# Two heads' half-array products of a linear attention issued in turn, and the whole-array products of its output put ahead of them

## What is computed

```python
def step(state, xs):
    qc, kc, vc, bc = xs
    o_inter = jnp.einsum('bhcd,bhde->bhce', qc * jnp.exp(bc), state)
    diff = bc[:, :, :, None, :] - bc[:, :, None, :, :]
    decay = jnp.exp(jnp.where(causal[:, :, None], diff, -jnp.inf))
    attn = jnp.einsum('bhid,bhjd,bhijd->bhij', qc, kc, decay)
    o_intra = jnp.einsum('bhij,bhje->bhie', attn, vc)
    b_last = bc[:, :, -1:, :]
    k_dec = kc * jnp.exp(b_last - bc)
    state = jnp.exp(b_last[:, :, 0, :])[..., None] * state + jnp.einsum('bhcd,bhce->bhde', k_dec, vc)
    return state, o_inter + o_intra
```

## Time and profile before

| | |
|---|---|
| median of 3 runs | 869.12 us (868.48 to 869.97) |
| profiled execution, its own time | 872.03 us |
| profiled execution, span of the trace | 870.2 us |
| mean granted TensorE clock in it | 0.993 |
| PE busy (share of span) | 848.4 us (97%) |
| DVE busy | 658.6 us (76%) |
| ACT busy | 556.8 us (64%) |
| POOL busy | 242.0 us (28%) |
| HBM traffic | 145 MB, 167 GB/s over the span |

### The profile page before, as it was taken

The page is one execution under the profiler, slowest core; times in us unless marked ns, Lnnn a source line. Parts: engine busy times, 40 slices in busy tenths (PEclk is TensorE's granted clock), DMA queues, the critical chain, the costliest instruction groups (busy, mean ns, idle before and its releaser), DMA issues.

```text
span 870.2 us, 16608 instructions
## 1 busy us (share of the span) xinstructions
PE 848.4 (97%) x6016; PEld 793.7 (91%) x6016; DVE 658.6 (76%) x1171; ACT 556.8 (64%) x1015; POOL 242.0 (28%) x252
## 2 busy tenths in 40 slices
PE   8999989999999999999999999999999999999996
PEld 8998989999999999999889888999998888888885
DVE  7998999996878897877766658837589766656552
ACT  7778969886746676666455685466646665555441
POOL 2387833332322153333101100010022152222111
PEclk9999999999999999999999999999999999999998
DMA  7665553534455476555656543335345465565731
GB/s 262 215 205 181 164 164 122 155 126 150 158 184 190 121 219 192 180 184 170 224 169 191 161 153 121 122 123 169 121 146 186 142 208 192 184 181 169 230 131 49
DMA packets 43024, 146.12 MB, mean 168 GB/s; under 512 B 4912, under 2 KB 7232, under 8 KB 42944
## 3 DMA queue, kind: packets, MB, share of 16 engines
q1 hardware_dynamic: 42336, 144.52, 52.6%
q10 hardware_dynamic: 608, 0.55, 0.2%
HBM read 144.00 MB, written 1.05 MB: 167 GB/s over the span
## 4 chain that ended last, share of the span: by engine, by line
PE 73%; DVE 12%; issue 4%; POOL 4%; ACT 4%; DMA 2%; DVEq 0%; SPq 0%; POOLq 0%; ACTq 0%
PE px L539 20%; PE px L543 12%; PE px L544 12%; PE px L545 12%; PE px L540 10%; DVE wlo L1400 4%; POOL CA L2011 4%; DMA raw<-ws 2%; PE px L588 2%; DVE px L1500 2%; PE px L610 1%; DVE hx L1417 1%; PE px L756 1%; ACT whi L899 1%; PE px L611 1%
## 5 line engine op out<-in xcount | busy, mean ns | idle before, releaser
L1400 DVE TENSOR_TENSOR wlo<-raw,whi 128x1024 fp32r<-128x1024 f32 x265 | 334.1, 1267 | 27.7 <-ACT whi L899 27.4
L899 ACT ACTIVATE whi<-raw 128x1024 fp32r<-128x1024 f32 x265 | 277.8, 1052 | 57.5 <-PE px L540 28.2
L543 PE MATMUL px<-hx,whi 128*128 128x256 f32 x1024 | 296.4, 289 | 2.8 <-DVE wlo L1400 1.6
L544 PE MATMUL px<-hx,whi 128*128 128x256 f32 x1024 | 290.1, 283 | 0.0
L545 PE MATMUL px<-hx,wlo 128*128 128x256 f32 x1024 | 290.0, 283 | 0.0
L543 PEld LDWEIGHTS px<-hx,whi 128*128 128x128 f32 x1024 | 196.7, 192 | 5.4 <-issue 2.8
L544 PEld LDWEIGHTS px<-hx,whi 128*128 128x128 f32 x1024 | 196.8, 192 | 0.4
L545 PEld LDWEIGHTS px<-hx,wlo 128*128 128x128 f32 x1024 | 196.6, 192 | 0.0
L2011 POOL TENSOR_TENSOR CA<-CA,ct 128x256 f32<-128x256 f32 x90 | 91.9, 1021 | 98.0 <-ACT ct L994 53.9
L539 PE MATMUL px<-fx,whi 128*128 128x512 f32 x330 | 115.6, 393 | 0.0
L539 PE MATMUL px<-hx,whi 128*128 128x512 f32 x320 | 113.4, 399 | 0.8 <-DVE wlo L1400 0.5
(11 more groups left out here) (315 smaller groups left out, 1378.7 us busy)
## 6 DMA issues: line engine op xcount, KB each, us to landing
raw<-ws SPq DMA_DIRECT2D x265, 512.0 KB, 3.6
tb<-tabs SPq DMA_DIRECT2D x16, 128.0 KB, 2.3
X<-xs SPq DMA_DIRECT2D x4, 256.0 KB, 3.7
raw<-ws SPq DMA_DIRECT2D x4, 256.0 KB, 5.0
out<-X SPq DMA_DIRECT2D x4, 256.0 KB, 2.4
vc<-vecs SPq DMA_DIRECT2D x1, 315.5 KB, 6.4
msk<-lmask ACTq DMA_DIRECT2D x1, 256.0 KB, 2.7
ug<-pos ACTq DMA_DIRECT2D x1, 128.0 KB, 3.9
```

The source lines that it names most:

```text
L543: e.matmul(b[:, 0:S], H, xh, start=first, stop=False)
L544: e.matmul(b[:, 0:S], H, xl, start=False, stop=False)
L899: e.activation(whi[:, n % NSL, :], raw[:, n % NRAW, :], ACT.Copy).then_inc(s_hi, 1)
L1400: e.tensor_tensor(wlo[:, n % NSL, :], raw[:, n % NRAW, :], whi[:, n % NSL, :], ALU.subtract).then_inc(s_lo, 1)
```

## The change

Only PE's program changes, in three of the helpers above. In `products` the loop over `par` goes inside, so that the two halves of the array are addressed in turn, matmul by matmul. In `chunk_sums` the order is written out: (p_, ci) = (0,0), (0,1), (1,0), (1,1), (0,2), (1,2). In `linear_out` the 8 whole-array matmuls of both `par` go first, and then the 12 half-array ones follow, with `par` changing at every matmul. Semaphore updates stay on the last matmul of what they announce. The number of instructions, their operands and their banks are the same.

```diff
-                for par in range(2):
-                    o = 64 * par
-                    for i in range(4):
-                        p_, t = i // 2, i % 2
+
+                for i in range(4):
+                    p_, t = i // 2, i % 2
+                    for par in range(2):
+                        o = 64 * par
                         if n == 0:
                             m = e.matmul(bs[par][:, i * P:i * P + P], gk[o:o + 64, p_, t * P:t * P + P],
...
-                for ci in range(3):
+                for p_, ci in ((0, 0), (0, 1), (1, 0), (1, 1), (0, 2), (1, 2)):
                     o, t = 64 * (ci % 2), ci // 2
-                    for p_ in range(2):
-                        m = e.matmul(bs[ci][:, p_ * S:p_ * S + S], kd[o:o + 64, t, p_ * P:p_ * P + P],
-                                     gv[o:o + 64, t, p_ * S:p_ * S + S], start=(p_ == 0), stop=True, skip_group_check=True)
-                    m.then_inc(s_cu, 1)
+                    m = e.matmul(bs[ci][:, p_ * S:p_ * S + S], kd[o:o + 64, t, p_ * P:p_ * P + P],
+                                 gv[o:o + 64, t, p_ * S:p_ * S + S], start=(p_ == 0), stop=True, skip_group_check=True)
+                    if p_ == 1:
+                        m.then_inc(s_cu, 1)
...
                 for par in range(2):
-                    b, o = bs[par], 64 * par
+                    b = bs[par]
                     for p_ in range(2):
                         h = 2 * p_ + par
                         for t in range(2):
                             e.matmul(b[:, p_ * S + t * P:p_ * S + t * P + P], gv[:, t, h * P:h * P + P],
                                      at[:, par, (2 * p_ + t) * P:(2 * p_ + t) * P + P],
                                      start=(p_ == 0 and t == 0), stop=False, skip_group_check=True)
-                    for p_ in range(2):
-                        for ci in range(1, 4):
-                            m = e.matmul(b[:, p_ * S + ci * 64:p_ * S + ci * 64 + 64], gs[o:o + 64, ci - 1, p_, :],
+                for p_ in range(2):
+                    for ci in range(1, 4):
+                        for par in range(2):
+                            o = 64 * par
+                            m = e.matmul(bs[par][:, p_ * S + ci * 64:p_ * S + ci * 64 + 64], gs[o:o + 64, ci - 1, p_, :],
                                          qL[o:o + 64, p_, ci * 64:ci * 64 + 64], start=False, stop=True,
                                          skip_group_check=True)
-                    m.then_inc(s_go, 1)
+                            if p_ == 1 and ci == 3:
+                                m.then_inc(s_go, 1)
```

## The result

The changed kernel takes 864.88 us (median of 6 runs, 863.64 to 865.93) against 868.86 us for the kernel before (6 runs, 868.16 to 872.45) measured beside it: ratio 0.9949, 95% interval 0.9933 to 0.9965. A repeat in a later session gave 0.9959 (0.9943 to 0.9975), with medians of 866.66 and 868.90 us. One of its twelve executions took 1169.47 us at a mean granted clock of 0.654 and is left out of that ratio. The forecast was 865.2 us, 0.45% faster.

A forecast was written before the change was run, and what follows sets the result against it. PE was taken as the bound, busy 97% of the span. Savings of 2.24 (`products`) + 0 (`chunk_sums`) + 1.67 (`linear_out`) = 3.9 us off 869.12 gave 865.2 us; forecast's own range 864.4 to 866.0, wider range 863.2 to 867.6.

The forecast's parts named there:

- The price of a pass and the pairing: In `products`, a pass takes a 0.112 us slot; both halves run together, 8 slots not 12, saving 0.45 us a call.
- The first two calls bring nothing: `products(0)` and `products(1)`: 0.9 us of PE's gain lost waiting for DVE; wait before `products(2)` about 1.26 us.
- From `products(2)` on the gain stays: Five later `products` calls keep 0.448 us each, 2.24 us; tightest is `products(6)`, with about 1.1 us left.
- `chunk_sums` at nothing: In `chunk_sums` upper passes already run beside lower ones, so reordering gains nothing; bounds 0.22 us more or less.
- `linear_out`, 3.36 us: `linear_out` falls from 5.03 to 3.36 us, saving 1.67, with 24 half-array passes in 12 slots.
- The clock: Half-clock stretch from 529.86 us, costing 1.5 us, expected to stay; rivals: gone, 863.7 us (0.12); another, 866.7 us (0.10).
- Draining at each switch: Rival: each switch of half on the path costs 0.09 us, 43 times, without pairing; about 875 us, chance 0.04.
- no pairing: Rival: alternating halves gives one pass a slot or little better, 12 slots a `products` call; 868.8 us, chance 0.07.
- Strict program order: Rule for MATMUL starts: old `products` call 16 slots, 1.8 us; change saves about 5.8 us in all; given no chance.

## Why the prediction held

- *The price of a pass and the pairing.* Right: 8 slots in place of 12, and the kernel with turns of 1 to 4 matmuls shows the reach of four passes that I had read from the earlier trace rows. The saving is 0.46 to 0.49 us a call, not 0.448: the upper half's first pass now shares the slower first slots with the lower half's too.
- *The first two calls bring nothing.* Right, and shown alone: ratio 1.0009, wait 1.28 us where about 1.26 was forecast. What is lost there is 1.0 us and not 0.9, since `products(0)`, with moving operands of 128 columns, saves 0.55 us.
- *From `products(2)` on the gain stays.* Right in the sum, 2.4 us against 2.24. The tightest case was not `products(6)`, as I wrote, but `products(3)`: in the change its queries are ready at 530.80 (below, the timeline of DVE) and PE comes at 531.51, 0.7 us later.

```profile
530.38 0.42 DVE L1840 TENSOR_TENSOR go<-gq,eb 128x256 f32<-128x256 f32 x1
```

  In the earlier trace rows that place was covered by the stretch at half clock, which held PE back, and I took its slack from a profile that had it. The two runs that moved calls on PE ran into just this.
- *`chunk_sums` at nothing.* Right, 1.92 us both times.
- *`linear_out`, 3.36 us.* Right, 3.37 (forecast saving 1.67, measured 1.66).
- *The clock.* "So I expect the same half-speed stretch" was wrong for the profiled execution: its profile has neither that stretch nor the one near 120 us, and a changed number of stretches was among the prediction's own signs of being wrong. The price was right, 1.49 us against 1.5. The argument from the sum of idle and half-array time, 2.3 us both ways, does not hold: with that sum the same the stretch was there in one profile of the change and not in the other. I should have asked how often it comes rather than whether.
- *The nearness of the number.* 864.88 us lies 0.3 us from the forecast, and that is partly luck. One stretch more or less is worth 1.5 us, and in the repeat the medians were 866.66 and 868.90 us, 2.2 us apart, while the ratio gives 3.6 us. What does not depend on it is the saving in the passes, 4.08 us against the forecast 3.9.
- *Draining at each switch, and no pairing.* Neither: 24 passes in turns take 1.49 us (562.26 to 563.75), as twelve of one half did (1.48). The 0.09 us that the draining rival starts from is the way from half to whole array and not, as written, from whole to half: the five passes from 567.24 are half-array ones with a whole-array one behind the earlier trace rows.
- *Strict program order.* With turns of four matmuls a call takes 1.53 us in place of the 1.8 that sixteen slots need. The Trainium skill, "TensorE: Matmul & The Clock Gate", Part 3, says that MATMULs start in strict program order. For products of different halves the trace disagrees with that again.

## What to carry to other kernels

The fp32 matmuls here that fill only the lower or the upper 64 rows run side by side if the program offers the other half's pass within about four passes, so order such matmuls in turns, or at most in pairs (in `products` and `linear_out` each half has a bank of its own; a shared one was not tried). Keep whole-array matmuls together, apart from them. Before adding up such savings, strike out those in front of a wait for another engine: here 1.0 of 3.4 us of `products` was lost there, and it took a reordering on DVE, not on PE, to remove that wait without a new one. Differences between two single profiles (6.7 us here) can hold stretches of half clock that have nothing to do with the change (two of them here, 1.5 us each); compare the distances between marked instructions.

## What was not expected of the hardware

Entering the half array and leaving it again costs 0.34 us (3.71 against 3.37 us), as much as three passes. And the stretch at half clock behind `products(2)` starts 1.4 to 2.0 us after that call begins when it comes at all (529.86 against 527.82 before, 528.17 against 526.54 in the repeat, 529.02 against 527.57 with the first two calls in turns); it was in none of the four profiles with a wait of 0.21 us or less there. Four profiles are too few to say that the shorter wait prevents it, so that stays open.
